# Moving the weight buffers and the rounded activations to other offsets in SBUF in a two-layer trunk step on one core

## The reference, cut to what matters

```python
for l in range(2):
    sh1, sc1, g1, sh2, sc2, g2 = adaln(cvec, ada_w[l], ada_b[l])      # silu(c) @ (1024 x 6144)
    h = rmsnorm(x, norm1_g[l]) * (1 + sc1) + sh1
    mix = mixer_ab(h, w_in, conv_w, w_out, attend) if l == 0 else fourier_mix(h, fourier_w)
    x = x + g1 * mix
    h = rmsnorm(x, norm2_g[l]) * (1 + sc2) + sh2
    ff = swiglu(h, ffn_w1, ffn_w3, ffn_w2) if l == 0 else moe(h, ...)  # 2816 wide; 8 experts, top 2, 3584 wide
    x = x + g2 * ff
return rmsnorm(x, final_g)
```

## Time and profile before

| | us |
|---|---|
| median of 3 runs | 1526.41 (1526.12 to 1530.75) |
| the profiled execution, its own time | 1526.19 |
| its span, first to last instruction | 1524.4 |
| mean granted TensorE clock | 0.979 of full |

### The profile page before, as it was taken

One profiled execution on the slowest core, in us unless ns is written; L12 is line 12 of the kernel. 1 busy time (PEld: TensorE's weight loads), 2 busy tenths in 40 slices (PEclk: granted clock), 3 DMA queues, 4 the chain that ended last, 5 costly groups with the idle time before them and its releaser, 6 DMA issues.

```text
span 1524.4 us, 21169 instructions
## 1 busy us (share of the span) xinstructions
PE 1466.1 (96%) x8125; PEld 1237.7 (81%) x8125; DVE 1140.8 (75%) x1026; ACT 902.0 (59%) x716; POOL 19.0 (1%) x36
## 2 busy tenths in 40 slices
PE   7898899999898999999999999999999999999997
PEld 4787699999576788888888888888888888888885
DVE  3558465554544788888888888888879888888886
ACT  2343343332323677777677777677777777766774
POOL 1000000000000000000000000000000000000000
PEclk9899999999898999999999999999999999999999
DMA  9893776554687799899899999989989999998990
GB/s 345 317 318 100 257 241 192 170 192 139 249 307 261 275 368 375 297 370 374 319 349 367 349 331 370 369 300 369 367 309 369 364 348 332 368 376 292 379 355 30
DMA packets 203391, 463.35 MB, mean 304 GB/s; under 512 B 7572, under 2 KB 48696, under 8 KB 197192
## 3 DMA queue, kind: packets, MB, share of 16 engines
q1 hardware_dynamic: 202552, 460.84, 83.7%
q0 software_dynamic: 784, 1.75, 0.4%
HBM read 460.98 MB, written 1.57 MB: 303 GB/s over the span
## 4 chain that ended last, share of the span: by engine, by line
PE 91%; DVE 5%; ACT 2%; issue 1%; DMA 1%; SPq 0%; DVEq 0%; POOL 0%; ACTq 0%; POOLq 0%
PE ps L429 88%; PE ps L827 2%; ACT w_hi L990 1%; PE ps L508 1%; DVE w_lo L1166 1%; DVE hT L1242 1%; DMA tok<-in_x_sample 0%; DVE rstd L1236 0%; DMA raw<-in_ffn_w 0%; PE ps L442 0%; ACT arena L1123 0%; DVE w_lo L1479 0%; DVE xT L1403 0%; ACT hT L1014 0%; DVE tok L1207 0%
## 5 line engine op out<-in xcount | busy, mean ns | idle before, releaser
L429 PE MATMUL ps<-w_hi,rnd 128*128 128x512 f32 x2720 | 862.7, 393 | 2.1 <-DVE rnd L1473 2.1
L1479 DVE TENSOR_TENSOR w_lo<-raw,w_hi 128x2048 fp32r<-128x2048 f32 x335 | 763.9, 2291 | 126.9 <-ACT w_hi L1080 126.4
L1080 ACT ACTIVATE w_hi<-raw 128x2048 fp32r<-128x2048 f32 x336 | 643.9, 1919 | 187.2 <-PE ps L429 187.2
L429 PEld LDWEIGHTS ps<-w_hi,rnd 128*128 128x128 f32 x2720 | 511.5, 188 | 111.4 <-issue 3.2
L429 PE MATMUL ps<-w_lo,rnd 128*128 128x512 f32 x1360 | 530.2, 390 | 0.0
L429 PE MATMUL ps<-rnd,w_hi 128*128 128x256 f32 x1632 | 301.4, 287 | 6.1 <-DVE rnd L1250 5.6
L429 PEld LDWEIGHTS ps<-w_lo,rnd 128*128 128x128 f32 x1360 | 256.0, 188 | 51.0
L429 PEld LDWEIGHTS ps<-rnd,w_hi 128*128 128x128 f32 x1632 | 257.6, 194 | 15.4 <-issue 13.6
L429 PE MATMUL ps<-rnd,w_lo 128*128 128x256 f32 x816 | 232.6, 285 | 0.0
L1166 DVE TENSOR_TENSOR w_lo<-raw,w_hi 128x2048 fp32r<-128x2048 f32 x53 | 121.3, 2291 | 110.9 <-ACT w_hi L990 110.8
L990 ACT ACTIVATE w_hi<-raw 128x2048 fp32r<-128x2048 f32 x53 | 101.1, 1910 | 147.1 <-PE ps L429 88.4
(11 more groups left out here) (123 smaller groups left out, 515.3 us busy)
## 6 DMA issues: line engine op xcount, KB each, us to landing
raw<-in_moe_w SPq DMA_DIRECT2D x336, 1024.0 KB, 6.7
raw<-in_ada_w SPq DMA_DIRECT2D x48, 1024.0 KB, 7.1
raw<-in_ffn_w SPq DMA_DIRECT2D x33, 1024.0 KB, 5.4
raw<-in_w_in SPq DMA_DIRECT2D x12, 1024.0 KB, 7.6
raw<-in_w_out SPq DMA_DIRECT2D x4, 1024.0 KB, 9.2
raw<-in_fourier_w SPq DMA_DIRECT2D x4, 1024.0 KB, 8.5
out<-tok SPq DMA_DIRECT2D x4, 256.0 KB, 2.0
arena<-dft_constants POOLq DMA_DIRECT2D x1, 640.0 KB, 4.2
```

The costliest lines, as they stand in the source:

```text
L429: return pe.matmul(out, lhsT, rhs, start=first, stop=last, **kw)
L1080: act.activation(w_hi[:, slot, :], raw[:, m % RAW, :], ACT.Copy).then_inc(hi_done, 1)
L1479: dve.tensor_tensor(w_lo[:, slot, :], raw[:, m % RAW, :], w_hi[:, slot, :].bitcast(F32), ALU.subtract).then_inc(lo_done, 1)
```

## The change

Three small tensors (`router_bias` 32 bytes, `idx` 64, `most` 4) are declared ahead of `raw`, so that `raw` begins at byte 16640, a multiple of 256, and `w_hi` and `w_lo` with it. `rnd` is moved to the place behind `w_lo`, also a multiple of 256, and made 64 elements longer. Its regions begin 48 elements (192 bytes) into it in the dense part and 16 elements (64 bytes) into it for the experts. No instruction is added or removed, and no instruction's shape changes. The tensors behind `rnd` move with it: `xT`, `hT`, `tok` and the constants, 128 bytes past a multiple of 256 before, come to lie on one, and `arena` stays 128 past one.

```diff
+LINE = 64
+DENSE_AT, MOE_AT = 48, 16
...
+    router_bias = sb("router_bias", [P, EXPERTS])
+    idx = sb("idx", [P, NG, 8], U32)
+    most = sb("most", [P, 1], I32)
     raw = sb("raw", [P, RAW, HALF])
     w_hi = sb("w_hi", [P, STAGE, HALF], F32R)
     w_lo = sb("w_lo", [P, STAGE, HALF], F32R)
+    rnd = sb("rnd", [P, 4 * KT * T + LINE], F32R)
...
-    router_bias = sb("router_bias", [P, EXPERTS])
...
-    idx = sb("idx", [P, NG, 8], U32)
-    most = sb("most", [P, 1], I32)
     arena = sb("arena", [P, 9728])
-    rnd = sb("rnd", [P, 4 * KT * T], F32R)
...
-    free[0] = 0
+    free[0] = DENSE_AT
     h_r = [region(KT, T, of=rnd) for _ in range(2)]
     mix_r = [region(KT, T, of=rnd) for _ in range(2)]
-    free[0] = 2 * KT * T
+    free[0] = DENSE_AT + 2 * KT * T
     ffn_r = [region(2, 4, T, of=rnd) for _ in range(2)]
     f_r = h_r
-    free[0] = 0
+    free[0] = MOE_AT
     hg_r = [region(KT, SLOTS, of=rnd) for _ in range(2)]
     gt_r = [region(2, 4, SLOTS, of=rnd) for _ in range(2)]
```

## The result

The changed kernel takes 1534.92 us (median of 20 runs) where the kernel before takes 1527.25: ratio 1.0053, 95% interval 1.0039 to 1.0067. (One of the 20 of the kernel before took 4922 us; it does not move the median.) I had forecast 1461 and a range up to 1530.

The account below looks back on a forecast made before the run. The prediction took TensorE's matmul count times pitch to bound the kernel. Gains of 66.4 us, 43.9 of them in the experts, less 1.3 for late blocks, took 1526.19 to 1461 us; the range was 1452 to 1530.

Parts of the forecast that it names:

- What bounds the kernel: Feed-forward layer and all eight experts: time is the number of matmuls times their pitch; TensorE holds 91% of the chain.
- The excess is not a fixed price of the matmul: Three-part matmuls at full clock: 32 cycles over the columns come from moving and weight reads colliding in SBUF.
- Rival 2: All three-part matmuls: 32 cycles are the price of switching weights, whatever the address; 1526 us, within 3; chance 0.20.
- The step that failed: Dense part and experts: stationary minus moving at 64 bytes cuts the excess in both, to pitches of 109.2 and 215.8 ns.
- The experts' term: Experts: 4032 matmuls, each falling from 226.7 to 215.8 ns, gain 43.9 us.
- The output projection: Output projection: 192 matmuls gain 2.1 us, half counted, 1.0, because the chain then waits for feed-forward weights.
- The convolution's nothing: Convolution's three parts, 288 matmuls: no gain, as attention's softmax chain covers them; 3.1 us more without that cover.
- The feed-forward layer's term: Feed-forward layer: 1584 matmuls, each falling from 120.0 to 109.2 ns, gain 17.1 us, all of it counted.
- What would be late next: Experts' first slices: ScalarE's blocks come late, giving back 1.3 us; VectorE still fits, DMA queue let fit at no cost.
- Rival 1: Half a gain: a smaller collision keeps 16 of 32 cycles, or the DMA queue binds; 1475 to 1520 us, chance 0.20.
- Rival 3: Experts' inner loop: at 64 bytes reads stay in the worse stand seen after a break, 237 ns; 1567 us, chance 0.14.
- The tests that I had named: Changed profile: predicted expert and feed-forward pitches; values' 48 matmuls keeping 226.7 ns while experts fall would show distance counts.

Follow-up runs that it names:

- t3: The changed kernel with the experts' down matmuls cut in two, 256 moving columns each instead of 512, same offsets; 1530.52 us in one run.
- u1: The changed kernel with the experts' activations at 0 instead of 64, dense part as changed; 1518.08 us, ratio 0.994 to the kernel before.
- m1: The kernel before with only the dense part's rounded activations moved 192 bytes later in `rnd`; 1514.71 us, ratio 0.9938 to the kernel before.

## Why the prediction was wrong, point by point

- *What bounds the kernel.* Right. The time is matmuls times pitch over the feed-forward layer and the experts, and it moved by that: 15.0 us gained ahead of the first expert, 20.6 lost after. The rest of the 10.3 us between the profiled spans is mostly the start, 5.0 us later, which varies from one execution to another.
- *The excess is not a fixed price of the matmul.* Right. It depends on the operands' offsets and is gone at 1.2 GHz, before and after. Rival 2, no effect, is refuted.
- *The step that failed* is the one between: that the same distance of 64 bytes must do the same in both parts, and that the same excess at two lengths belongs to the matmul and not to its columns. It was 32 cycles at both lengths only because the distance was 0 in both. At 64 the number of streamed columns decides: 16 (or 27) for 256, 48 for 512. The rows of before had a single distance in them and could not show that; the forecast should have carried the sign of the experts as an open question of its own, with more than half of the three-part matmuls and 2/3 of the stake on it.
- *The sum.* The experts' term, +43.9 us, measured -20.6. That is less than 4032 x 6.6 ns = 26.6: just after a break the pitch was 237 ns before as well, and a slice of 72 lost 0.43 us. The dense terms had the right sign, 22.5 us forecast and 15.0 measured. Three were too large, because the excess fell to 16 cycles and not to the 6 of the plain float32 rows: feed-forward layer 17.1 forecast, 10.4 measured; Fourier projection 2.1 against 1.2; queries, keys and values 2.3 against 1.3 (44.44 to 43.13 us in one piece). The output projection, counted half at 1.0, gave 2.3 from its start to the feed-forward layer's (44.43 to 42.16 us). The convolution's nothing held: from the end of queries, keys and values to the output projection 57.8 us became 57.5. The feed-forward layer's term also hangs on something that the prediction did not have: of the six kernels with it at distance 64 five took 16 cycles in their profiled executions, this one too, and t3 took 26.7, where the term is 193.07 - 189.46 = 3.6 us.
- *What would be late next.* Not put to the test: no block came late, since the experts slowed. The spare time grew, ScalarE's waits for TensorE from 187.2 to 201.7 us.
- *Rival 1*, half a gain, has in it the excess that 256 columns took, 16 of the 32 cycles; it put it on the experts too, and these went the other way.
- *Rival 3* is what happened in the experts, by its place and by what shows in the timeline: the pitch stays near the one after a break and does not settle. That it is a stand of two reads is its reading, which no run shows. Its price, 41 us, took the pitch right after a break (237 ns) for the settled one (233.3), and it gave the dense part no gain of its own. Against it I had argued that a shift moves off a coincidence and not onto one; the table shows that for 512 columns 0 is the best of all places tried. Its chance, 0.14, was too low for a mechanism that no row spoke against.
- *The Trainium skill's rule.* By the Trainium skill's "SBUF — State Buffer", "Who interferes with whom", TensorE's two read ports are independent, and nothing should have changed. The trace differs: with the same instructions the pitch is 113.3 or 120.0 ns, 226.7 or 233.3, by offset alone. The measurement decides for the time; that it is these ports or what is behind them that collide is argued from the half clock and was not shown.

The tests that I had named did tell it: the 48 matmuls of the values, at distance 192, went to 37.4 cycles and not to the experts' 48, which pointed to distance, and the dense and the expert pitch going apart pointed to what else differs.

## What to carry to other kernels

The float32r matmuls of this kernel carry 16 to 48 cycles of excess each at full clock, and the offset of the stationary operand against the moving one, modulo 256 bytes, narrows it to one value or two; a shift of one region by 192 bytes was worth 0.6% here, without an instruction more. The good distance depends on the number of columns streamed (64 bytes for 256 columns, 0 for 512, of those tried), so it is set for each loop by itself and checked in the timeline by the distance between starts, not by busy time. It is checked in every long stretch, since 256 columns at 64 bytes had two pitches here. When one excess is seen at two shapes under one condition, that says nothing of the two under another.

## What was not expected of the hardware

- At 2.4 GHz the excess never fell under 16 cycles for 256 columns or 32 for 512 in a settled stream; at 1.2 GHz it was 0 in both kernels (213.3 ns for 256 columns). The Trainium skill, "TensorE: Matmul & The Clock Gate", section "Back-to-back issue gap", has 518 cycles for 512 columns at full clock as the isolated gap; the best of these three-part products is 544.
- Eight bytes matter: 56 and 72 bytes gave 33 and 32 cycles at 256 columns, 64 gave 16 (or 27).
- One placement can settle in two ways, 16.0 or 26.7 cycles, and a stretch without a break keeps the one it took. At distance 64 the Fourier projection ran at 16 cycles in the changed kernel (30.86 us for its piece) and at 26.6 in u1 (31.68 us), with the same offsets; in m1 its first 96 matmuls ran at 26.7 and the other 96 at 16.0. The whole feed-forward layer ran at 16 in the changed kernel and at 26.7 in t3 (182.65 and 189.46 us), and m1's queries and keys ran at 26.7. At distance 0 no settled stretch of 256 columns had anything but 32. What decides between the two was not found, nor how often the slower pitch comes, since each kernel has one profiled execution. Nor was it found why the number of columns turns the sign, since 256 and 512 columns both are whole multiples of 256 bytes.
